# Latent attention and the S5 branch: query chunks made one step ahead, and three blocks joined into one with waits by name

## What is computed

```python
# first block, per layer: latent attention of 4 heads
q = (rms_norm(c_q, q_norm_w) @ w_uq)            # per head 128 nope + 64 rope
q = concat([q_nope, apply_rope(q_rope)])
k_nope, v = split(rms_norm(c_kv, kv_norm_w) @ w_ukv)
s = einsum('bqhd,bkhd->bhqk', q, concat([k_nope, k_rope])) * scale
o = einsum('bhqk,bkhd->bqhd', softmax(s), v)

# second block
proj = h @ w_in                                  # all branches' inputs
x_re, x_im = associative_scan(a, B u)            # S5: states of 16 groups
y = gelu(C x + d * u); y = y * sigmoid(y @ glu_w + glu_b)
gates = sigmoid(proj[gates])                     # 32 tiles, 4 per output tile
```

## Time and profile before

| | |
|---|---|
| median of 3 runs | 3359.33 us (3356.55 to 3360.12) |
| the profiled execution | 3359.92 us, its span 3358.1 us |
| PE busy | 3196.7 us, 95% |
| PEld busy | 2726.0 us, 81% |
| DVE busy | 2058.2 us, 61% |
| ACT busy | 1010.1 us, 30% |
| POOL busy | 938.9 us, 28% |

### The profile page before, as it was taken

One profiled execution on the slowest core, in us unless ns is written; L12 is line 12 of the kernel. 1 busy time (PEld: TensorE's weight loads), 2 busy tenths in 40 slices (PEclk: granted clock), 3 DMA queues, 4 the chain that ended last, 5 costly groups with the idle time before them and its releaser, 6 DMA issues. The chain is left out here.

```text
span 3358.1 us, 41800 instructions
## 1 busy us (share of the span) xinstructions
PE 3196.7 (95%) x17082; PEld 2726.0 (81%) x17082; DVE 2058.2 (61%) x2422; ACT 1010.1 (30%) x1456; POOL 938.9 (28%) x617
## 2 busy tenths in 40 slices
PE   8998999999899999999998999999999999999997
PEld 7997888999788898878867996666777787888875
DVE  5535664444466634556456554655676766897788
ACT  2113332101233320000022221555432644344643
POOL 3320001233000032333224322100142443555575
PEclk9999999999999999999999999999999999999998
DMA  3120000211100013323331003211361454455443
GB/s 135 45 65 9 21 1 20 77 45 45 33 21 8 1 45 135 130 93 97 103 126 54 1 1 111 72 42 38 117 227 59 146 172 156 132 183 171 147 158 119
DMA packets 111758, 282.12 MB, mean 84 GB/s; under 512 B 15010, under 2 KB 20770, under 8 KB 111552
## 3 DMA queue, kind: packets, MB, share of 16 engines
q1 hardware_dynamic: 107104, 263.19, 23.4%
q10 hardware_dynamic: 4464, 16.25, 1.2%
HBM read 237.37 MB, written 41.42 MB: 83 GB/s over the span
## 5 line engine op out<-in xcount | busy, mean ns | idle before, releaser
L3639 PE MATMUL psum<-x,w_hi 128*128 128x512 f32 x2016 | 627.0, 392 | 8.3 <-DVE x L3610 3.1
L199 POOL CAST w_hi<-w_raw 128x1024 fp32r<-128x1024 f32 x116 | 126.2, 1088 | 1795.9 <-PE psum L212 1112.0
L3639 PEld LDWEIGHTS psum<-x,w_hi 128*128 128x128 f32 x2016 | 379.1, 189 | 93.1 <-issue 6.9
L3639 PE MATMUL psum<-x,w_lo 128*128 128x512 f32 x1008 | 393.4, 390 | 0.0
L3524 POOL TENSOR_TENSOR w_lo<-w_sum,w_hi 128x512 fp32r<-128x512 f32 x180 | 252.9, 1412 | 330.0 <-ACT w_hi L3518 330.0
L727 PE MATMUL psum<-h,w_hi 128*128 128x512 f32 x1024 | 328.1, 402 | 15.2 <-PEq L126 11.5
L203 POOL TENSOR_TENSOR w_lo<-w_raw,w_hi 128x1024 fp32r<-128x1024 f32 x116 | 301.9, 2602 | 16.4 <-DVE y L1533 7.2
L727 PEld LDWEIGHTS psum<-h,w_hi 128*128 128x128 f32 x1024 | 190.2, 192 | 63.1 <-issue 21.9
L3639 PEld LDWEIGHTS psum<-x,w_lo 128*128 128x128 f32 x1008 | 190.0, 189 | 39.8
L212 PE MATMUL psum<-hn_hi,w_hi 128*128 128x348 f32 x864 | 188.9, 327 | 16.5 <-DVE hn_lo L409 15.1
L727 PE MATMUL psum<-h,w_lo 128*128 128x512 f32 x512 | 202.7, 396 | 0.0
(11 more groups left out here) (464 smaller groups left out, 6491.4 us busy)
## 6 DMA issues: line engine op xcount, KB each, us to landing
w_raw<-in_w_mlp SPq DMA_DIRECT2D x169, 256.0 KB, 2.9
norm_factor<-in_w_mlp SPq DMA_DIRECT2D x87, 256.0 KB, 2.8
w_raw<-in_w_mlp SPq DMA_DIRECT2D x42, 512.0 KB, 3.4
w_raw<-in_w_in SPq DMA_DIRECT2D x36, 512.0 KB, 3.4
w_raw<-in_w_gates SPq DMA_DIRECT2D x32, 512.0 KB, 4.2
gates_kept<-gate_stage SPq DMA_DIRECT2D x64, 256.0 KB, 2.1
gates<-gates_kept SPq DMA_DIRECT2D x32, 512.0 KB, 3.3
w_raw<-in_w_out SPq DMA_DIRECT2D x24, 512.0 KB, 3.5
```

The source lines that it names most:

```text
L199: self.core.nc.gpsimd.tensor_copy(self.hi[:, g % 2], self.raw[:, g % 2]).then_inc(self.hi_done, 1)
L3639: last = self.core.nc.tensor.matmul(out, one[:, k, :], other[:, k, :], start=(group == 0 and k == 0 and part == 0), stop=(group == second ...
```

## The change

Two things, which don't touch each other.

1. `head_jobs` gets another table. The third query chunk's `qr` moves from step 5 to 3 and its `qn` from 3 to 4; the next head's first `qr` and `qn` from 8 to 5 and 6, its second chunk's from its own step 0 to step 8 of this head; `kn` from steps 5 and 6 to 0 and 7. The steps before the first tile start at -9 instead of -4, so that this table's early jobs are in them. The reload of a head's weights waits for `qn` instead of `qr`.
2. One phase is held open around `branch_products`, `s5_states` and S5's outputs. What the two ends of a block did is now done by waits on the engines that need them: `BranchesEnded` names the stores of `stage`, of `h_all`, and the read-out of the last two accumulators; TensorE waits for S5's rows itself; and ahead of S5's outputs it waits for four semaphores of the states.

```diff
-            s5.sync_end(sp)
+    return BranchesEnded(core.weights, x.g0 + N_PROJ2, stored, h_stored)
+
+class BranchesEnded:
+    def __init__(self, weights, g_end, stored, h_stored):
+        self.weights, self.g_end, self.stored_rows, self.h_stored = weights, g_end, stored, h_stored
+    def stored(self, eng):
+        for b in range(2):
+            eng.wait_ge(self.stored_rows[b], 16 * ((N_PROJ2 + 1 - b) // 2))
+    def h_kept(self, eng):
+        eng.wait_ge(self.h_stored, 16 * KT)
+    def read_out(self, eng):
+        for g in (self.g_end - 2, self.g_end - 1):
+            eng.wait_ge(self.weights.acc_free[g % 2], g // 2 + 1)
...
-    jobs = {0: [("qr", n, 1), ("qn", n, 1)], 1: [("pv", n - 1, 2)], 2: [("v", n, 0), ("v", n, 1)],
-            3: [("v", n, 2), ("qn", n, 2)], 4: [("pv", n, 0)], 5: [("qr", n, 2), ("kn", n + 1, 0)],
-            6: [("kn", n + 1, 1), ("kn", n + 1, 2)], 7: [("pv", n, 1)], 8: [("qr", n + 1, 0), ("qn", n + 1, 0)]}
+    jobs = {0: [("kn", n + 1, 0), ("kn", n + 1, 1)], 1: [("pv", n - 1, 2)], 2: [("v", n, 0), ("v", n, 1)],
+            3: [("v", n, 2), ("qr", n, 2)], 4: [("qn", n, 2), ("pv", n, 0)], 5: [("qr", n + 1, 0)],
+            6: [("qn", n + 1, 0)], 7: [("kn", n + 1, 2), ("pv", n, 1)], 8: [("qr", n + 1, 1), ("qn", n + 1, 1)]}
...
-    steps = range(-4, tiles + 2)
+    steps = range(-NH, tiles + 2)
...
-                sp.wait_ge(job_done, number["qr", n - 2, 2] + 1)
+                sp.wait_ge(job_done, number["qn", n - 2, 2] + 1)
...
+            together = ExitStack()
+            together.enter_context(core.phase())
...
-                s5_branch(core, io, gates, masks, vecs, ybr, s5, [(masks[:], io["masks"])])
+                s5_branch(core, io, gates, masks, vecs, ybr, s5, ended, [(masks[:], io["masks"])])
+            together.close()
...
-    def sync_end(self, sp):
-        sp.wait_ge(self.u_in, 16 * 2 * (SC + 1))
+    def wait_rows(self, eng):
+        eng.wait_ge(self.u_in, 16 * 2 * (SC + 1))
...
         @block.tensor
         def _(pe):
+            pe.wait_ge(g_saved, 4)
+            pe.wait_ge(l_saved, 4)
+            pe.wait_ge(toe_in, 16 * SC)
+            pe.wait_ge(dve_step, 2 * 16 * SHIFTS)
...
         @block.sync
         def _(sp):
+            ended.stored(sp)
+            ended.h_kept(sp)
             for dst, source in coming:
...
             gates.sync(sp, 9)
-            sp.wait_ge(toe_in, 16 * SC)
...
         @block.gpsimd
         def _(pool):
+            ended.stored(pool)
+            ended.h_kept(pool)
...
             gates.tensor(pe, 2 * KT)
+            ended.read_out(pe)
+            x.wait_rows(pe)
             pe.wait_ge(rest_in, 16 * len(coming))
...
+            ended.stored(dve)
             for _half in range(2):
                 gates.vector(dve)
```

More of the change, by code:

```diff
@@ L1420, in second_block @@
             s5 = S5Inputs(core)
+            together = ExitStack()
+            together.enter_context(core.phase())
             with core.scope():
                 stage, last_sq = core.sb("stage", [P, 2, T2]), core.sb("last_square", [P, TP])
-                branch_products(core, io, hi, lo, stage, last_sq[:], h_all, final_w, r, ones, s5, [(vecs[:], io["vec2"])],
+                ended = branch_products(core, io, hi, lo, stage, last_sq[:], h_all, final_w, r, ones, s5, [(vecs[:], io["vec2"])],
                                 comes_first)
@@ L2717, in vector_in, with s5_branch @@
         tt(out, s1, s2, ALU.add if part else ALU.subtract)
-def s5_branch(core, io, gates, masks, vecs, ybr, inputs, coming):
+def s5_branch(core, io, gates, masks, vecs, ybr, inputs, ended, coming):
     nc = core.nc
@@ L2733, in s5_branch @@
     gates.two = True
-    s5_states(core, io, gates, masks, x, finT, toe, ks, [(glu[:], io["s5_glu_w"])] + coming)
+    (g_saved, l_saved, dve_step, toe_in) = s5_states(core, io, gates, masks, x, finT, toe, ks, ended,
+                                                      [(glu[:], io["s5_glu_w"])] + coming)
     ug, hout = x.ug, x.hout
@@ L2818, in _, with s5_states @@
                 gates.vector(dve)
-def s5_states(core, io, gates, masks, x, finT, toe, ks, coming):
+def s5_states(core, io, gates, masks, x, finT, toe, ks, ended, coming):
     nc = core.nc
@@ L2926, in _ @@
             gates.vector(dve)
+    return g_saved, l_saved, dve_step, toe_in
 def output_and_mlp(core, io, gates, ybr, r, vecs, ones, ident):
```

## The result

The kernel now takes 3330.72 us (median; 3327.83 to 3337.89) against 3358.01 (3356.55 to 3360.12): a ratio of 0.992, 95% interval 0.9905 to 0.9936. The sign was right, the size was wrong, and the range was too narrow. The profiled execution took 3330.66 us, with a span of 3328.9.

The account below looks back on a forecast made before the run. TensorE, busy 95% of the span, was taken as the bound, so only its stands and low clock could be won. S5's 13.6 us plus latent attention's 3.0 made 16.6: 3342.7 against 3359.33 us, range 3336 to 3351.

Parts of the forecast that it names:

- S5, 13.6 us: S5's two block ends: gains of 6.8 and 7.4 us less 0.6 given back; bounds 14.2 and 9.3.
- Both seams: Before S5's gates and outputs: TensorE's stands of 4.6 and 4.8 us go, with clock losses of 2.2 and 2.6.
- The masks: At S5's first seam: masks land near 1517.7, transposes need them at 1519.0, 1.3 us of margin.
- The given-back term: Semaphore clears moved behind S5's outputs and to RWKV's first block cost some 0.3 us each, together 0.6.
- Inner heads, 1.7 us each: Latent attention's first three heads: waits of 3.4 us go, 1.7 come, gain 1.7 a head, 5.1 a layer.
- Last head, 1.9 us lost: Latent attention's last head, without successor: bare steps wait 6.3 us against 4.4 before, 1.9 lost a layer.
- The clock, one more fall a layer: Behind the last head's second tile in each latent layer: one new low-clock stretch, 1.7 us lost; bounds 0 and 3.4.
- A: Rival: latent attention gives nothing, its waits replaced and the clock dropping twice; 3346.7 us, or 3350; chance 0.17.
- B: Rival: S5's first seam, its stand moves to the late masks; 3347.7 us; chance 0.05.
- C: Rival: slower, paired waits at seventh and eighth tile pull the clock down inside latent heads; 3366 us; chance 0.01.
- D: Rival: a block's end stays between S5's parts, so only 2.6 to 3 us are won; 3356 us; chance 0.01.
- E: Rival: no new fall of the clock in latent attention, 3.4 us more gained; 3339.3 us; chance 0.34.

Follow-up runs that it names:

- the join alone: Kernel before with only S5's three blocks joined into one, job table as before: 3345.85 us against 3359.71 (0.9958).
- Experiments 1 and 2: 1: kernel before with the new job table alone, 3348.0 us, or the joined blocks alone, 3345.85; 2: changed kernel again, 3329.64, and kernel before, single run 3366.76.
- experiments 5 and 6: Unread products in TensorE's long waits: 5, changed kernel 3333.55 us, kernel before 3360.86, `qn`-first kernel 3330.9; 6, resized 3324.18, kernel before at one end 3350.45, 3351.93.
- Experiment 4: Changed kernel with the last head's query chunks placed as before, 3330.71 us (0.9908); with the opening as before, 3331.48 (0.9918).
- experiment 6: Changed kernel, `qn` first, unread products sized to its waits: 3324.18 us; kernel before with them in the opening alone, 3350.45, or last head's end alone, 3351.93.
- the swap: Changed kernel with `qn` ahead of `qr` in steps 5 and 6; timed only with other job moves, 3330.38 us, or unread products, 3330.9 and 3324.18.
- experiment 3: Changed kernel with jobs moved into its bare steps and `qn` ahead of `qr` in steps 5 and 6: 3330.38 us (0.9912).

## Why the prediction was wrong, by its own steps

**S5, 13.6 us: right.** Measured 13.8 in the profile and 13.9 with the join alone. Both seams went, stand and clock together. The masks were in time: 10.89 us from gates to transposes, as forecast with 10.9. The given-back term was too large: RWKV's first block takes 59.29 us (1675.20 to 1734.49) where it took 59.25 (1707.96 to 1767.21), although SyncE now clears 65 semaphores: its last clear starts at 1733.4, and ScalarE's last piece ends at 1732.98 + 1.02 = 1734.0. Forecast 0.3, measured 0.04: the 65 clears took 3.6 us from first to last (1729.8 to 1733.4), not 4.4. The 15 clears of the seam before are in the 13.8: PE's wait there went from 2.34 to 2.65, 0.3 as forecast.

**Inner heads, 1.7 us each: right, a little small.** 0.22 at the seventh tile (forecast 0.35 between issues, 0.1 in the row), 0.72 at the eighth (0.8), 0.23 at one value product of three. Period of a head 62.1, against 64.0: 1.9.

**Last head, 1.9 us lost: near in its waits, too dark in its sum.** The bare steps wait 1.57, 1.67 and 1.89, forecast 1.9 for each. The idle time of a layer fell by 2.9, but part of what is left lies beside low clock; without any low clock the table is worth 4.8 a layer against my 3.2; three heads at 1.93 are 5.8, so opening and last head together lose 1.0, not 1.9.

**The clock, one more fall a layer: this step failed.** "The last head's step 0 now makes a wait of that size where none was [...]: I take one more fall in each layer, 1.7." The sign was wrong. Experiments 1 and 2 show two low stretches fewer in layers of like start, and the price list makes this 2.3 us gained where 1.7 were taken off: 4.0 of the 5.6 us that a layer was off, 8 of 11 in the kernel. The reasoning behind it, that low clock follows a wait of 1.88 and does not follow waits of 1.06, took one example for a rule. In the changed kernel a wait of the same 1.88 stands at 297 us and three of 1.67 to 1.96 near 515, and 290 to 531 us is granted 1.00. What the runs put in its place: idle time does bring the low clock (with unread products in the long waits, experiments 5 and 6 have no low stretch inside eight layers of three kernels, up to the last microsecond), but a given wait brings it in one layer and not in the next, which goes with where the first low stretch falls, and a low stretch that lies beside waits can cost nothing. My bounds for this term ran from no new fall to two. Only the lower end of the range had one fall fewer, and its 3336.5 doesn't come out of its words: 3339.3 less 1.7 is 3337.6. Four us a layer were not in it. That is why the range failed too: an edit that takes away 3 of 23 us of idle can take away falls, and I had counted that as certain for S5's seams and hardly at all here.

Trainium skill, TensorE: Matmul & The Clock Gate, section "What's actually happening": the chip watches activity in its own rhythm, free of the program, so one kernel shows different numbers of slow matmuls from run to run. By that rule the trace agrees: the changed kernel's layers have 1, 2, 3, 2, 2 and 2 low stretches with the same long waits, and layers of like start have like counts. Weighed ahead of the result, it would have told me to forecast a count with a spread, not one fall at one named wait. The section "A second HAM failure mode: psum-queue depth-cycling", weighed in the prediction, is borne out by half: the short waits of inner heads (0.2 to 1.1 us) stay at full clock, so the row that I chose against it was right for them. But its direction, fewer stops and less low clock, is what happened at a layer's opening and end.

**Rivals.** A (latent attention gives nothing), B (masks), C (slower) and D (not joined) did not occur. E, no new fall, was the nearest, and still 8.6 us too high (3339.3).

**What stays open.** Which of the table's moves took the second stretch of the opening and the second near the end away. Experiment 4 points to the opening by one pair of layers of like start; in experiment 6 filling the opening alone also left none or one of the two near the end. To settle it would take, for each kernel, more layers of like start than two profiles give. Nor is there a run of the swap without fillers, so in the whole kernel's time the two are not told apart; the layers do it, 1.2 us for the swap and some 3.3 for the clock.

## What to carry to other kernels

Take the count of low-clock stretches as something an edit changes in both directions, and price it from both sides. Compare such counts only between stretches whose first low stretch begins equally far in. When TensorE's idle time falls, put the removal of existing falls in the range. Before costing a fall, look whether it lies beside a wait that ends by another engine; there it can be free. And a job only fills a bare step if the step it leaves had more than its chain needs: in experiment 3 no move between steps gained, only the swap of `qr` and `qn`.

## What the chip showed that was not expected

- Products that nobody reads, sized to end before a wait does, keep the granted clock of a layer at 1.00 and make the kernel faster: 3324.18 us with the swap, 0.9881 (0.9865 to 0.9898) of the kernel before against 0.992 (0.9905 to 0.9936) for the change alone, of which the swap's 1.2 us a layer are a part. Oversized by 3 us they gave it all back.
- The same program's layers differ by up to 2.9 us (261.92 to 264.86) through the clock alone, and by nothing (259.58 and 259.58) without low stretches or where the first begins equally far in (264.03 five times, 0.01 apart). A single profile can't tell a 2 us edit of such a part.
- SyncE's clears cost little while another engine ends the block: 53 more of them changed RWKV's first block by 0.04 us.
